# Layer norms of a fused two-block kernel, made by halves of the tokens

## The reference

```python
def layer_norm(x, g, b):
    xf = x.astype(jnp.float32)
    mu = jnp.mean(xf, -1, keepdims=True)
    var = jnp.mean(jnp.square(xf - mu), -1, keepdims=True)
    return ((xf - mu) * lax.rsqrt(var + LN_EPS)).astype(x.dtype) * g + b
```

## Time and profile before

| | |
|---|---|
| median of three runs | 2152.41 us |
| profiled execution, its own time | 2150.55 us |
| span of the profiled execution | 2148.7 us |
| PE busy | 2049.4 us, 95% |
| DVE busy | 1266.3 us, 59% |
| ACT busy | 316.5 us, 15% |
| POOL busy | 196.3 us, 9% |
| mean granted PE clock | 0.975 of full speed |

### The profile page before, as it was taken

How to read it: one execution, slowest core, us unless ns; L and a number is a source line. 1 busy time by engine, 2 the same in 40 slices (tenths; PEclk the granted TensorE clock), 3 DMA queues, 4 the chain that set the end, 5 groups by cost and what they waited for, 6 DMA issues and landing times.

```text
span 2148.7 us, 34899 instructions
## 1 busy us (share of the span) xinstructions
PE 2049.4 (95%) x14212; PEld 1576.7 (73%) x14212; DVE 1266.3 (59%) x2460; ACT 316.5 (15%) x611; POOL 196.3 (9%) x244
## 2 busy tenths in 40 slices
PE   6999899989999998999999988999999998999998
PEld 3577774433333335999988777999999996779997
DVE  4667543312111114888757575988798876656773
ACT  2033111111111111000002611000000001710001
POOL 0000012222222320000010000000000000000000
PEclk9999999999999999999999999999999998999998
DMA  9865649999999999565873202665856573225541
GB/s 391 315 234 215 260 172 413 414 383 408 392 407 354 407 394 420 206 240 203 295 294 107 98 1 79 237 248 202 317 205 228 205 277 139 81 79 177 177 156 42
DMA packets 92975, 530.23 MB, mean 247 GB/s; under 512 B 24236, under 2 KB 24492, under 8 KB 33296
## 3 DMA queue, kind: packets, MB, share of 16 engines
q1 hardware_dynamic: 58176, 413.49, 49.9%
q0 software_dynamic: 33776, 112.25, 14.4%
q10 hardware_dynamic: 864, 2.25, 0.3%
HBM read 619.13 MB, written 24.12 MB: 299 GB/s over the span
## 4 chain that ended last, share of the span: by engine, by line
PE 85%; DMA 9%; DVE 4%; issue 1%; SPq 1%; ACT 1%; DVEq 0%; ACTq 0%
PE ps L1377 33%; PE ps L1272 10%; PE ps L1307 5%; DMA ring<-in_exp_up 5%; PE ps L1531 4%; PE ps L1098 4%; PE ps L1432 4%; PE ps L1395 3%; PE ps L961 3%; PE ps L987 2%; PE ps L1510 1%; DMA ring<-in_exp_down 1%; PE ps L1245 1%; DMA ring<-moe_rows 1%; DVE x_streams L2363 1%
## 5 line engine op out<-in xcount | busy, mean ns | idle before, releaser
L1377 PEld LDWEIGHTS ps<-h,ring 128*128 128x128 f32 x4480 | 500.9, 192 | 0.2
L1377 PE MATMUL ps<-h,ring 128*128 128x128 f32 x4480 | 500.9, 275 | 0.0
L2363 DVE TENSOR_TENSOR ring<-ring 128x512 f32<-128x512 f32 (+4 forms) x416 | 355.4, 872 | 15.5 <-issue 3.5
L1272 PE MATMUL ps<-ring,h 128*64 128x512 f32 (+1 forms) x1536 | 303.4, 610 | 15.0 <-DMA ring<-in_exp_up 13.5
L1272 PEld LDWEIGHTS ps<-ring,h 128*64 128x64 f32 (+1 forms) x1536 | 100.8, 132 | 204.6 <-issue 203.7
L2451 DVE SCALAR_TENSOR_TENSOR ring<-ring,ada_acc 128x1024 f32<-128x1024 f32 x152 | 179.6, 1222 | 52.0 <-DMA ring<-in_mod_w 35.2
L2766 DVE COPY hidden<-ps 128x256 f32<-128x256 f32 x42 | 17.8, 424 | 269.9 <-PE ps L1284 263.3
L1377 PE MATMUL ps<-ring 128*128 128x128 f32 x1464 | 166.7, 275 | 0.0
L1377 PEld LDWEIGHTS ps<-ring 128*128 128x128 f32 x1464 | 165.4, 192 | 0.2
L1307 PE MATMUL ps<-ring,hidden 128*64 128x512 f32 (+1 forms) x768 | 153.4, 597 | 1.8 <-DVE hidden L2766 1.6
L2238 POOL DMA_DIRECT2D ring<-in_mod_w x72 | 38.7, 538 | 1002.1 <-DVE ring L2451 728.1
(11 more groups left out here) (473 smaller groups left out, 2361.3 us busy)
## 6 DMA issues: line engine op xcount, KB each, us to landing
ring<-in_exp_up SPq DMA_DIRECT2D x128, 1024.0 KB
ring<-in_mod_w POOLq DMA_DIRECT2D x72, 1024.0 KB, 6.7
ring<-in_exp_down SPq DMA_DIRECT2D x64, 1024.0 KB
ring<-in_ffn_gate SPq DMA_DIRECT2D x44, 1024.0 KB, 4.9
ring<-in_ffn_up SPq DMA_DIRECT2D x44, 1024.0 KB, 6.4
ring<-in_ffn_down SPq DMA_DIRECT2D x32, 1024.0 KB, 5.0
ring<-in_ada_late POOLq DMA_DIRECT2D x16, 1024.0 KB, 6.1
ring<-in_hyb_in SPq DMA_DIRECT2D x16, 1024.0 KB, 6.3
```

The lines of the kernel that those rows point to most:

```text
L1272: last = mm(b[z * e:z * e + z, :], xt[:, 2 * half + k // 2, k % 2, z * e:z * e + z], w[:, k, :], start=half == 0 and k == 0, stop=half == ...
L1377: ins = mm(dst, a[:, kt, :], b[:, kt, :], start=first and n < 2 and kt == 0, stop=last and n > 4 and kt == half - 1)
L2363: return V.tensor_tensor(out_, a, b, op)
```

## The change

Tokens are taken in two halves of 128, called h = 0 and h = 1.

- y3 is made in two banks, y3a for the first half of the tokens and y3b for the second (`last_down`, `last_pair`). In an FFN all three chunks of weights are read for y3a, then again for y3b; a slot is freed in the second pass. In `hout` the first pass makes blocks 0 to 3 of y3a alone; all of y3b comes in the second.
- After the first four blocks of y3b, PE makes the sums of half 0 (`norm_sums(..., 0)`): 12 instructions of 128 tokens with a full 128x128 block of ones, so that each sum stands on every partition at once. `fold` and `spread_row` are no longer used in these norms, and the two packed rows and their spreading go.
- The opening products go half by half (`opening`): 128 instructions of 128 tokens. After feature blocks 0 and 1 of half 0, PE makes the sums of half 1.
- DVE adds one halving operation to each of the two partial sums, and then for each half in turn: both products of y3, mean, square, variance, reciprocal, and the whole of that half's new input (`new_half`). The products of y3b stand behind all of half 0's new input. The modulation items stay ahead of y3a.
- The second unit of each FFN is interleaved (`second_up`): gate's and up's first two terms, then the wait for `turned`, then the third, then the rest.
- ACT squares groups 6 and 7 of a half in one instruction. In ln5 it scales half 0 before it comes to half 1, and the output is stored as one half and then four quarters of the other.
- POOL's three waits go to the corresponding group of half 1.

```diff
+            def last_pair(tag, k, w, a, z):
+                for h in range(2):
+                    if h == 1 and z < KT:
+                        continue
+                    lo = 0 if h else a
...
+                    for kt in range(lo, z):
+                        for m in range(2):
+                            last = mm(b[:, token_half(m)], w[:, kt, m * P:(m + 1) * P], MIX[:, kt, token_half(h)],
+                                      start=kt == 0 and m == 0, stop=kt == KT - 1 and m == 1)
+                        if h == 1 and kt == KT // 2 - 1:
+                            norm_sums(k, tag, 0)
...
+                def last_down(h):
+                    b = open_bank(f"{tag}_y3{'ab'[h]}")
+                    for c, n in enumerate(DOWN_KT):
...
+                        for kt in range(n):
+                            for m in range(2):
+                                ins = mm(b[:, token_half(m)], w[:, kt, m * P:(m + 1) * P], HIDA[:, k0 + kt, token_half(h)],
+                                         start=c == 0 and kt == 0 and m == 0, stop=c == len(DOWN_KT) - 1 and kt == n - 1 and m == 1)
+                            if h and c == 0 and kt == n // 2 - 1:
+                                norm_sums(LN_OF[norm], f"{tag}_y", 0)
+                        if h:
+                            ins.then_inc(S("down_done"), 1)
...
+            def norm_sums(k, ytag, h):
+                tag = f"ln{k - 1}"
+                b = open_bank(f"{tag}_sum{h}")
+                pe.wait_ge(S("summed"), 2 * k - 1)
+                mm(b[:, 0:P], ONES, SUMS[0][:, 0, token_half(h)], start=True, stop=False)
+                wait(pe, uses[f"{ytag}3{'ab'[h]}"].free)
                 for kt in (6, 7):
+                    last = mm(b[:, 0:P], ONES, AXS[:, kt, token_half(h)], start=False, stop=kt == 7)
+                full(last, f"{tag}_sum{h}")
+                b = open_bank(f"{tag}_sq{h}")
+                pe.wait_ge(S("summed"), 2 * k)
+                mm(b[:, 0:P], ONES, SUMS[1][:, 0, token_half(h)], start=True, stop=False)
+                pe.wait_ge(S("squared_part"), 4 * k - 1 + h)
+                for kt in (6, 7):
+                    last = mm(b[:, 0:P], ONES, SQ[:, kt, token_half(h)], start=False, stop=kt == 7)
+                full(last, f"{tag}_sq{h}")
+
+            def opening(parts, k, ytag):
...
+                for h in range(2):
+                    for kt in range(KT):
...
+                                wait(pe, ready(k, h, n))
...
+                        if h == 0 and kt == 1:
+                            norm_sums(k, ytag, 1)
...
+            def new_half(k, h):
+                x, mean, rinv = AXS[:, :, token_half(h)], MEAN[:, token_half(h)], RR[:, token_half(h)]
+                for n, (a, z) in enumerate(GROUPS if k < 6 else LAST_GROUPS):
+                    if n >= 2:
+                        link(tt_(x[:, a:z], x[:, a:z], over(mean, z - a), AD))
+                    ins = tt_(x[:, a:z], x[:, a:z], over(rinv, z - a), M)
+                    if k < 6:
+                        link(ins)
+                        for kt in range(a, z):
+                            ins = ts_(U_IN[:, kt, token_half(h)], x[:, kt], n_a[:, kt:kt + 1], M, n_b[:, kt:kt + 1], AD)
+                    tell(ins, *ready(k, h, n))
...
-                    tell(tt_(SUMS[n], SUMS[n], src[:, 4:6], AD), "summed", 2 * k - 1 + n)
+                    link(tt_(SUMS[n], SUMS[n], src[:, 4:6], AD))
+                    tell(tt_(SUMS[n][:, 0], SUMS[n][:, 0], SUMS[n][:, 1], AD), "summed", 2 * k - 1 + n)
                 if f"{ffn}_end" in MODS:
                     mods(f"{ffn}_end", 0, MODS[f"{ffn}_end"][2])
...
+                for h in range(2):
+                    y3 = f"{ytag}3{'ab'[h]}"
+                    b = full(y3)
...
+                    for kt in (6, 7):
+                        ins = stt(x[:, kt], b[:, token_half(kt - 6)], g1c[:, kt:kt + 1], x[:, kt], M, AD)
+                    freed(ins, y3)
+                    b = full(f"{tag}_sum{h}")
+                    freed(ts_(mean, b[:, 0:P], -1.0 / D, M), f"{tag}_sum{h}")
+                    link(tt_(squared, mean, mean, M))
+                    b = full(f"{tag}_sq{h}")
+                    freed(stt(rinv, b[:, 0:P], 1.0 / D, squared, M, SU), f"{tag}_sq{h}")
+                    for a, z in GROUPS[:2]:
+                        link(tt_(x[:, a:z], x[:, a:z], over(mean, z - a), AD))
+                    root = ROOT[f"{tag}_{h}"]
+                    dve.wait_ge(S("rinv"), root)
+                    tell(V.reciprocal(rinv, rinv), "recip", root)
+                    new_half(k, h)
```

More of the change, by code:

```diff
@@ L763, in build @@
         ei_c = small(248, 1)
+        LN_OF = {f"ln{k - 1}": k for k in range(1, 7)}
         y_of = lambda kt: PS[:, 4 + kt // 2, (kt % 2) * T:(kt % 2 + 1) * T]
@@ L768, in build @@
         MASKED, WEIGHED, RANKED, SORTED_, CHOSEN, BLANKED, SELECTED, ADDED = range(1, 9)
-        ROOT = {n: k + 1 for k, n in enumerate(["first", "heads_a", "heads_r", "second", "third", "ln0", "l2_q", "l2_k", "delta", "ln1", "ln2", "ln3", "latent", "ln4", "ln5"])}
+        ROOT = {n: k + 1 for k, n in enumerate(["first", "heads_a", "heads_r", "second", "third", "ln0_0", "ln0_1", "l2_q", "l2_k", "delta", "ln1_0", "ln1_1", "ln2_0",
+                                          "ln2_1", "ln3_0", "ln3_1", "latent", "ln4_0", "ln4_1", "ln5_0", "ln5_1"])}
         block = ctx.enter_context(nc.Block())
@@ L1361, in _, with fast @@
             spread_row("third_row", STAT)
-            def fast(banks, w, sums, turned, src, k0, half, sums_at, first=True, last=True):
+            def fast(banks, w, sums, turned, src, k0, half, sums_at, first=True, last=True, steps=range(7)):
                 x, y = (PS[:, b, :] for b in banks)
@@ L1379, in fast, with units @@
                 return ins
-            def units(tag, phase, norm):
+            def units(tag, phase, norm, before=None):
                 q = ph[tag]
                 def first_up():
-                    parts = (q.L0, uses[f"{tag}_gate0"]), (q.L0 + 1, uses[f"{tag}_up0"])
-                    for L, u in parts:
-                        wait(pe, u.prev.free)
+                    parts = [(q.L0 + m, f"{tag}_{name}0") for m, name in enumerate(("gate", "up"))]
+                    if phase:
+                        opening(parts, phase, before)
+                        return
+                    banks = [open_bank(name) for _, name in parts]
+                    for L, _ in parts:
@@ L1436, in units @@
                 first_up()
-                pe.wait_ge(S("turned"), q.turn0 + 1)
-                for e in range(1, q.n):
+                second_up()
+                for e in range(2, q.n):
                     up(e)
-                for p in range(4):
+                for p in range(3):
                     for c in range(len(DOWN_KT)):
@@ L1444, in units @@
                             shift(norm, f"{tag}_y")
[L1446 to L1457, removed]
-                for kt in (6, 7):
-                    pe.wait_ge(S("squared_part"), 4 * k + kt - 7)
-                    last = fold(c, SQ[:, kt, :], False, kt == 7)
-                full(last, f"{tag}_sq")
-                wait(pe, uses[f"{tag}_sum"].free)
-                spread_row(f"{tag}_mean", MEAN_F)
-                pe.wait_ge(S("recip"), ROOT[tag])
-                spread_row(f"{tag}_rinv", STAT)
@@ L1473, in _ @@
             units("ffn0", 0, "ln0")
-            layer_norm("ln0", 1, "ffn0_y")
             def indexer():
@@ L1732, in _ @@
             project_out("hout", 2, "ln1", halves=((0, 4), (4, KT)), between=delta_norm, first=uses["dsa_o3"].free)
-            layer_norm("ln1", 2, "hout")
-            units("ffn1", 2, "ln2")
-            layer_norm("ln2", 3, "ffn1_y")
-            units("ffn2", 3, "ln3")
-            layer_norm("ln3", 4, "ffn2_y")
-            pair_up(("ml0", "ml1"), L_MLA, 4)
+            units("ffn1", 2, "ln2", "hout")
+            units("ffn2", 3, "ln3", "ffn1_y")
+            opening([(L_MLA + n, f"ml{n}") for n in range(2)], 4, "ffn2_y")
             L = L_MLA + 2
@@ L1809, in _ @@
             project_out("mout", 3, "ln4")
-            layer_norm("ln4", 5, "mout")
-            units("ffn3", 5, "ln5")
-            layer_norm("ln5", 6, "ffn3_y")
+            units("ffn3", 5, "ln5", "mout")
+            norm_sums(6, "ffn3_y", 1)
         even_k0 = {"dsa": 0, "mla": 4}
```

201 lines of the change are left out of this document (108 added, 93 removed).

## The result

The changed kernel takes 2171.32 us (median of 4 runs, 2170.37 to 2171.96), the kernel before beside it 2154.11 (2150.96 to 2155.82): ratio 1.008, interval 1.0067 to 1.0092. It is slower, as forecast, but by 17.2 us and not by 9.4; 2171.3 lies above the range's upper end of 2169.

A forecast was written before the change was run, and what follows sets the result against it. PE, busy for 95% of the span, was taken as the bound. 11.3 + 0.9 - 0.4 - 2.4 = +9.4 us brought the profiled 2150.55 to 2159.9, for a median 2161; range 2151 to 2169.

The forecast's parts named there:

- ln0, ln2, ln3: In y3b PE waits 6.7 us for DVE, still in modulation items; loss 12.3 us, 11.3 after 1.0 of relief.
- the 1.8 us of clock: Low granted clock expected behind the stall inside y3b, in each of ln0, ln2 and ln3: 1.8 us.
- The relief of 1.0 us for the third load: SP's loads move behind y3b, so the third modulation load has less beside it: 1.0 us saved over three norms.
- rival 1: In ln0, ln2, ln3 DVE's wait for the third modulation load vanishes: -1.1 us in all, 2151; chance 0.10.
- Rival 3: DVE reaches y3a in time, so all is hidden: -17 us in all, 2135; chance 0.06.
- the 36.6: PE's time from y3's start to the opening's end in an FFN's norm, if DVE were always on time: 36.6 us.
- ln1: Norm behind `hout`: PE stalls 3.4 us for y3b's products; equal at full clock, 1 us charged for clock: +0.9.
- ln4: Norm behind `mout`: same 3.4 us stall for y3b's products; -1.6, with 1.2 for the clock -0.4 us.
- ln5: Last norm, without modulation items: y3b ends 2.0 us later, but ACT's end comes sooner: -2.4 us.
- The rest, at nothing: `second_up`, DVE's unit 2 operands and POOL's later wait behind ln0 were taken as covered, at no cost.
- Rival 4: More low clock from frequent short idles, another 1.8 us in four norms: +16.6 us, 2169; chance 0.12.

The follow-up runs named there:

- the added operation: Changed kernel plus one DVE maximum operation of 128x1024 (1.2 us) behind ln0's modulation items: 2170.56 us, one run.
- both edits: Changed kernel with the third modulation item behind the norm (ln0, ln2, ln3) and y3b's products behind half 0's second group (ln1, ln4): 2145.48 us, ratio 0.9965 to before.

## Where the prediction held and where it failed

*ln0, ln2, ln3.* Right in place, and near in size: 3.7 (against the repeated executions of before; 2.8 against the profiled one), 4.8 and 3.8, together 11.3 to 12.3 for the 11.3 forecast. PE went on at 1568.76, 18.85 us behind the start of y3a, and the step had it at 1553.63, 18.31 behind. The wait was 6.84 us for 6.7, and the first 72 instructions behind it took 9.12 us for 8.04, which is most of the 1.8 us of clock that I had charged. The relief of 1.0 us for the third load came, and was larger, though not in ln2: DVE waited 3.11 us for 4.45 in ln0, 3.13 for 3.25 in ln2 and 3.14 for 3.84 in ln3, together 2.2 us less.

```profile
1071.18 1.22 DVE L2521 SCALAR_TENSOR_TENSOR ring<-ring,ada_acc 128x1024 f32<-128x1024 f32 x1 [3.11 <-DMA ring<-in_mod_w]
...
1788.14 1.23 DVE L2521 SCALAR_TENSOR_TENSOR ring<-ring,ada_acc 128x1024 f32<-128x1024 f32 x1 [3.14 <-DMA ring<-in_mod_w]
```

No run shows that SP's loads made the difference. With 3.1 us of wait left in each of the three, rival 1 is refuted. Rival 3 failed with it, and the experiments show what it lacked: with one item less ahead of y3a these norms take 37.4 us, near the 36.6 that the prediction had for a DVE that is on time.

*ln1.* The step that put it at +0.9 failed by size. The timelines of PE and DVE there:

```profile
1348.51 3.19 PE L1110 MATMUL ps<-h,ring 128*128 128x128 f32 x16
1351.62 2.02 PE L1552 MATMUL ps<-h,ring 128*128 128x128 f32 x16
...
1357.04 0.71 PE L1529 MATMUL ps<-x_streams,always 128*128 128x128 f32 x4 [3.17 <-DVE x_streams L2441]
...
1358.56 14.00 PE L1552 MATMUL ps<-h,ring 128*128 128x128 f32 x112
```

```profile
1346.24 0.61 DVE L2441 SCALAR_TENSOR_TENSOR x_streams<-ps,small,x_streams 128x128 f32<-128x128 f32 x2
...
1356.38 0.61 DVE L2441 SCALAR_TENSOR_TENSOR x_streams<-ps,small,x_streams 128x128 f32<-128x128 f32 x2
```

Less the shift of 11.95 us that stands ahead of `hout`, DVE adds y3a by 1334.9, as forecast; from there to the end of y3b's products it takes 10.1 us and not 9.1; the sums behind take 0.4 more; and the last 112 instructions take 14.00 us where 112 x 0.1117 is 12.51. That makes 1.0 + 0.4 + 1.5 = 2.9 later than the 1357.7 of the step, where the clock was charged at 1 of a possible 2. The place of the stall (behind feature block 1, 3.17 us for 3.4) was right, and moving y3b's products forward took it away.

*ln4.* With the latent block +0.4 for -0.4. The same stall, 3.2 us; `mout`'s low clock fell from 3.4 to 1.7 us and paid for part of it.

*ln5.* -2.3 for -2.4.

*The rest, at nothing.* This is the step that failed most. It named waits that might show in the hybrid block (POOL's, DVE's, PE's indexer) and found them covered, and they are: the changed kernel has no wait there that the kernel before has not. It took the granted clock of these 206 us of unchanged work to stay as it was, without a reason, though ln0 ahead of them takes another time. That cost 5.5 us: 15.4 us low for 8.5 is 6.8 us more, and one wait of 1.2 us that the block had before is gone beside it. Rival 4 had more clock as its price and 2169 as its time, but for another reason and in another place: it looked in the norms, where the stalls are. With 11.3 + 2.8 + 5.5 + 0.4 - 2.3 = 17.7 the account is closed.

The Trainium skill's passage behind rival 4 (TensorE: Matmul & The Clock Gate, A second HAM failure mode) speaks of short idles between groups of matmuls. At the indexer the traces agree only in part: score products with waits of 0.2 to 0.7 us stand in the low stretch in both kernels, but in the changed kernel the clock falls 1.4 us ahead of the first of these waits. The same waits go with 13.7 us of low clock there and with 10.2 with the added operation, so they alone don't decide how long it stays low.

What stays open is how the moment decides it. It isn't the absolute time: the block starts at 1101.04 us in the changed kernel's first trace and at 1098.79 in its second, with 15.4 us low in both. What the traces have in common is the distance from the end of ffn0's fast part (y0 to y2, which has no low clock in any trace) to the block: 44.9 to 45.2 us in the four with 15.4 us low; 37.4, 41.1 to 42.2 and 47.3 to 48.4 in the nine with 8.5. Three more have 37.4 and 11.9 us low; they are those with eight items, where PE waits some 6 us at the indexer. No run went through the distances between in small steps, so this is a finding and not an explanation.

## What to carry to other kernels

Work that is free on the helping engine is free only up to the deadline that the structure sets: before a hand-over is moved forward (here by half a block of products), list what stands ahead of it on the other engine and move that too, and make the sum for both edits together, since either alone showed nothing or a loss. Count the items again where the moved ones land: the eighth item ahead of the indexer cost 6.4 us (212.93 - 206.49), 3.4 us more low clock among it, and cost nothing once one went where DVE was idle. And let the range of a change of 0.5% hold the clock of the unchanged parts behind it: here 5 us came and went with the moment at which they start.

## What the runs showed of the hardware

The granted clock's low time in the hybrid block repeated from trace to trace, although the part ahead of ffn0 took between 875.1 and 878.8 us: 8.5 us in all three traces of before, and 15.4 us in all four of the changed kernel and its two variants that leave ln0's and the block's order alone. It then changed to 8.5 with 1.2 us of added work on another engine ahead of it. This is known of the traced executions only. The others show their time and mean clock, and these vary together: with both edits 2140.22 us at 0.980 and 2151.65 us at 0.975; no run shows in which stretches.

The price of halving an instruction of 256 tokens, 2 x 0.1117 - 0.216 us, held: the halved y3 and opening with their sums took 37.42 us in ln0, with no low clock, in each of the five traces with two items ahead of y3a, against the 36.6 worked out from rows.
